# A hybrid decoder step on one core: pooling projection ahead of the last o group, narrow last pooled group, reordered ends of stages

## What is computed

```
n1 = rmsnorm(h); q,f,v,g,u = split(n1 @ w_in)            # 5 x 1024 columns
o  = rmsnorm(hgrn2(silu(q), sigmoid(f), v)) * silu(g)    # 8 heads, state 128x128 each
pm = (window_means(u) - u) @ w_pool * pool_scale         # 4 groups of 256 channels, windows 2/4/8/16
h  = h + concat(o, pm) @ w_out                           # 2048 x 2048
gu = rmsnorm(h) @ w_gate_up                              # 2048 x 11264
h  = h + (silu(gu[:5632]) * gu[5632:]) @ w_down          # 5632 x 2048
e  = rmsnorm(p @ w_ple); h = h + sigmoid(h @ w_ple_gate) * e
y  = rmsnorm(h)                                          # and the new states and pooling buffers
```

## Time and profile before

| what | value |
| --- | --- |
| three runs | 1236.65, 1238.37, 1238.66 us; median 1238.37 |
| profiled execution | 1237.61 us, span 1235.7 us |
| granted TensorE clock, mean | 0.996 of full |
| PE busy | 1198.0 us, 97% |
| DVE busy | 786.2 us, 64% |
| ACT busy | 598.5 us, 48% |
| chain that ended last, by engine | PE 89%, DVE 6%, ACT 2%, DMA 2% |
| DMA | 232.86 MB, mean 188 GB/s |

### The profile page before, as it was taken

How to read it: one execution, slowest core, us unless ns; L and a number is a source line. 1 busy time by engine, 2 the same in 40 slices (tenths; PEclk the granted TensorE clock), 3 DMA queues, 4 the chain that set the end, 5 groups by cost and what they waited for, 6 DMA issues and landing times.

```text
span 1235.7 us, 27526 instructions
## 1 busy us (share of the span) xinstructions
PE 1198.0 (97%) x10761; PEld 1039.7 (84%) x10761; DVE 786.2 (64%) x1147; ACT 598.5 (48%) x741; POOL 27.8 (2%) x41
## 2 busy tenths in 40 slices
PE   4999999999999999999999999999999999999995
PEld 2889889888888878888888888888888888888885
DVE  3657767777867866565656656565664545455686
ACT  5643453445445665555555555555443434343442
POOL 2010101100000000000000000000000000000000
PEclk9999999999999999999999999999999999999998
DMA  5664756765556567565565756566364646555551
GB/s 195 210 200 151 228 157 201 223 183 168 198 170 219 155 204 222 168 217 190 185 220 159 221 166 218 189 186 221 136 240 158 216 170 217 175 205 190 191 144 71
DMA packets 172310, 232.86 MB, mean 188 GB/s; under 512 B 10178, under 2 KB 110761, under 8 KB 171976
## 3 DMA queue, kind: packets, MB, share of 16 engines
q1 hardware_dynamic: 167728, 220.30, 55.0%
q0 software_dynamic: 3024, 10.09, 2.8%
q10 hardware_dynamic: 1504, 1.70, 0.4%
HBM read 225.08 MB, written 7.43 MB: 188 GB/s over the span
## 4 chain that ended last, share of the span: by engine, by line
PE 89%; DVE 6%; ACT 2%; DMA 2%; issue 1%; DVEq 0%; ACTq 0%; SPq 0%
PE acc L1333 28%; PE acc L1335 28%; PE acc L1337 28%; DVE lo L768 2%; PE wrk L1443 2%; DMA raw<-in_w_in_dram 1%; ACT hi L506 1%; PE wrk L1360 1%; ACT big L543 0%; DVE hid L1212 0%; DMA raw<-in_w_gate_up_dram 0%; DVE nrm L1168 0%; DVE hid L1259 0%; DMA xe<-in_x_sample_dram 0%; PE wrk L1428 0%
## 5 line engine op out<-in xcount | busy, mean ns | idle before, releaser
L1333 PE MATMUL acc<-nrm,hi 128*128 128x264 f16 x2304 | 637.3, 277 | 3.8 <-DVE tg L1174 2.3
L768 DVE SCALAR_TENSOR_TENSOR lo<-raw,hi 128x1024 f16<-128x1024 f32 x414 | 497.2, 1221 | 222.4 <-ACT hi L506 219.0
L1335 PE MATMUL acc<-nrm,hi 128*128 128x264 f16 x2304 | 637.3, 277 | 0.0
L1337 PE MATMUL acc<-nrm,lo 128*128 128x264 f16 x2304 | 637.2, 277 | 0.0
L506 ACT ACTIVATE hi<-raw 128x1024 f16<-128x1024 f32 x414 | 423.8, 1051 | 327.4 <-PE acc L1337 111.1
L1333 PEld LDWEIGHTS acc<-nrm,hi 128*128 128x128 f16 x2304 | 227.5, 99 | 38.1 <-DVE tg L1174 2.6
L1337 PEld LDWEIGHTS acc<-nrm,lo 128*128 128x128 f16 x2304 | 228.4, 99 | 32.9
L1335 PEld LDWEIGHTS acc<-nrm,hi 128*128 128x128 f16 x2304 | 228.4, 99 | 32.7
L1333 PE MATMUL acc<-big,hi 128*128 128x264 f16 x720 | 198.8, 276 | 1.5 <-DVE hid L1212 1.5
L1335 PE MATMUL acc<-big,hi 128*128 128x264 f16 x720 | 198.8, 276 | 0.0
L1337 PE MATMUL acc<-big,lo 128*128 128x264 f16 x720 | 198.8, 276 | 0.0
(11 more groups left out here) (268 smaller groups left out, 725.2 us busy)
## 6 DMA issues: line engine op xcount, KB each, us to landing
raw<-in_w_gate_up_dram SPq DMA_DIRECT2D x352, 256.0 KB, 3.9
raw<-in_w_down_dram SPq DMA_DIRECT2D x88, 512.0 KB, 4.6
raw<-in_w_in_dram SPq DMA_DIRECT2D x80, 512.0 KB, 4.5
raw<-in_w_out_dram SPq DMA_DIRECT2D x32, 512.0 KB, 4.4
raw<-in_w_ple_gate_dram SPq DMA_DIRECT2D x32, 512.0 KB, 5.0
state<-in_state_hgrn_dram POOLq DMA_DIRECT2D x8, 512.0 KB, 6.9
out_new_hgrn_sample_dram<-state POOLq DMA_DIRECT2D x8, 512.0 KB, 5.0
xe<-in_x_prompt_dram SPq DMA_DIRECT2D x2, 1024.0 KB, 7.5
```

The costliest lines, as they stand in the source:

```text
L768: stt(lo[:, st.hl_slot(j), :], raw[:, st.raw_slot(j), :], WSCALE, hi[:, st.hl_slot(j), :], ALU.mult, ALU.subtract).then_inc(lo_done, 1)
L1333: mm(out, wh, x_hi[:, kt, :], start=first, stop=False)
L1335: mm(out, wh, x_lo[:, kt, :], start=False, stop=False)
L1337: last = mm(out, wl, x_hi[:, kt, :], start=False, stop=final)
```

## The change

- The pooling projection runs after three o groups instead of four; the fourth o group follows it (`MIX_BLOCKS`, the loads, PE's streams). `POOL_AT` is block 92, it was 96.
- In the tables of the front part `OSS_AT` goes from 70 to 73, `SAMPLE_ROOT_AT` from 71 to 74, `O_MIX_AT` from (68, 70, 72, 74) to (69, 71, 73, 75), `SAMPLE_MIX_AT` from 74 to 77.
- The last pooled group is narrow with 4 blocks: each of 8 row tiles by 128 columns, each finishing one tile. DVE and ACT evict, square and sum tile by tile inside the loop.
- `square_e(i)` runs in FFN groups 1 to 16 instead of 0 to 15.
- The down pass evicts its four tiles first and converts them afterwards.
- At the end, the transposes of y go to blocks 5, 6 and 7, the last four tiles of y are transposed after the pass, the sum over the squares is made in two parts (`ya` for the first 15 tiles, `ys` for the last), the stores are cut at 768 columns instead of 960, and y_sample is stored in 32 rows of 512 columns instead of 8 of 2048.

```diff
-BUF_AT, U_LAST_AT, OSS_AT = 44, (73, 81), 70
-RMS_AT, ROOT_AT, SAMPLE_ROOT_AT = 64, 65, 71
-O_NORM_AT, O_MIX_AT, SAMPLE_MIX_AT = (66, 67, 69, 71), (68, 70, 72, 74), 74
+BUF_AT, U_LAST_AT, OSS_AT = 44, (73, 81), 73
+RMS_AT, ROOT_AT, SAMPLE_ROOT_AT = 64, 65, 74
+O_NORM_AT, O_MIX_AT, SAMPLE_MIX_AT = (66, 67, 69, 71), (69, 71, 73, 75), 77
...
-MIX_BLOCKS += [(st, 0, j) for st in S_OUT_O for j in range(4)]
+MIX_BLOCKS += [(st, 0, j) for st in S_OUT_O[:-1] for j in range(4)]
+POOL_AT = len(MIX_BLOCKS)
 MIX_BLOCKS += [(S_POOL, 0, j) for j in range(2)]
-MIX_BLOCKS += [(st, 0, j) for st in S_OUT_P for j in range(4)]
+MIX_BLOCKS += [(st, 0, j) for st in S_OUT_O[-1:] + S_OUT_P for j in range(4)]
 MIX_END = len(MIX_BLOCKS)
-POOL_AT = IN_BLOCKS + 4 * OUT_GROUPS
...
-            for i, st in enumerate(S_OUT_P):
+            for i, st in enumerate(S_OUT_P[:-1]):
                 for j in range(4):
                     load(st, 0, j, std(w_out)(i, 4 + j))
+            for j in range(4):
+                load(S_OUT_P[-1], 0, j, w_out[:, 8:16, D - COLS + j * P:D - COLS + (j + 1) * P])
...
                 if st in S_OUT_P and j == 3 and st is not S_OUT_P[-1]:
                     square_h(S_OUT_P.index(st))
+                if st is S_OUT_P[-1]:
+                    square_h(OUT_GROUPS - 1, (j,))
                 split(*MIX_BLOCKS[b + AHEAD])
...
                     out_tiles(st, S_OUT_P.index(st))
                     out_sums(S_OUT_P.index(st))
+                if st is S_OUT_P[-1]:
+                    if j == 0:
+                        dve.wait_ge(acc_free, st.tile(0, 0))
+                    out_tiles(st, OUT_GROUPS - 1, (j,))
+                    if j == 3:
+                        out_sums(OUT_GROUPS - 1, (2, 3))
                 for c in range(QUADS):
                     quad_update(c, b - QUAD_AT[c])
                 split(*MIX_BLOCKS[b + AHEAD])
+                if st is S_OUT_P[-1] and j < 2:
+                    out_sums(OUT_GROUPS - 1, (j,))
                 for c in range(QUADS):
                     quad_rest(c, b - QUAD_AT[c])
...
-            with dve.Fori(0, KT) as i:
-                group(S_FFN, i, lambda: evac_ffn(i), between=lambda n: square_e(i) if n == 2 else None)
-            with dve.Fori(KT, S_FFN.groups - 1) as i:
+            group(S_FFN, 0, lambda: evac_ffn(0))
+            with dve.Fori(1, KT + 1) as i:
+                group(S_FFN, i, lambda: evac_ffn(i), between=lambda n: square_e(i - 1) if n == 2 else None)
+            with dve.Fori(KT + 1, S_FFN.groups - 1) as i:
...
             def evac_down(i):
                 for n in range(TPG):
                     wait_tile(dve, S_DOWN, i, n)
+                    h = tile_of(h_all, i, n)
+                    stt(h, acc[:, n, 0:TOK], C_FF, h, ALU.mult, ALU.add).then_inc(acc_free, 1)
+                for n in range(TPG):
                     h, nh = tile_of(h_all, i, n), tile_of(n_hi, i, n)
-                    stt(h, acc[:, n, 0:TOK], C_FF, h, ALU.mult, ALU.add).then_inc(acc_free, 1)
                     dve.wait_ge(acc_free, S_DOWN.tile(i, n) + 1)
                     ts(nh, h, HSCALE, None, ALU.mult).then_inc(down_chain, 1)
...
             gate_tile(last_gate, 0)
             split(S_GATE, last_gate, 7)
             gained((12,))
-            y_taken(0)
-            gate_tile(last_gate, 1)
-            gained((13,))
-            for c in (1, 2):
+            for n in (1, 2):
+                gate_tile(last_gate, n)
+                gained((12 + n,))
+            for c in range(3):
                 y_taken(c)
-            gate_tile(last_gate, 2)
-            gained((14,))
-            dve.wait_ge(gate_chain, Y_LAST // P * 3)
             gate_tile(last_gate, 3, summed=False)
+            ssp = rt[:, 8:11]
+            wait_job("ya")
+            ts(ssp[:, 0:2], bank("ya")[:, 0:2], 1.0 / D, EPS, ALU.mult, ALU.add)
+            link(drain(ts(ssp[0:NSAMP, 2:3], bank("ya")[0:NSAMP, 2:3], 1.0 / D, EPS, ALU.mult, ALU.add), "ya"))
             gained((15,))
-            y_taken(3)
-            wait_job("ys_2")
-            for n in range(3):
-                m = P if n < 2 else NSAMP
-                last = drain(ts(ss[0:m, n:n + 1], bank(f"ys_{n}")[0:m, 0:1], 1.0 / D, EPS, ALU.mult, ALU.add), f"ys_{n}")
-            link(last)
+            wait_job("ys")
+            stt(ss[:, 0:2], bank("ys")[:, 0:2], 1.0 / D, ssp[:, 0:2], ALU.mult, ALU.add)
+            link(drain(stt(ss[0:NSAMP, 2:3], bank("ys")[0:NSAMP, 2:3], 1.0 / D, ssp[0:NSAMP, 2:3], ALU.mult, ALU.add), "ys"))
...
+                if i == OUT_GROUPS - 1:
+                    pe.wait_ge(pd_ready, 2)
+                    stream(S_POOL, 0, pd_hi, pd_lo,
+                           layout=lambda j, n, kk: ((n // 2 * 2 + kk) * 256 + n % 2 * P, 2 * (2 * j + n // 2) + kk))
                 stream(st, 0, m_hi, m_lo, ready=out_ready if i == 0 else None,
                        woven=lambda j: in_jobs(IN_BLOCKS + 4 * i + j))
...
-            for st in S_OUT_P:
+            for st in S_OUT_P[:-1]:
                 stream(st, 0, m_hi, m_lo, layout=lambda j, n, kk: (kk * COLS + n * P, 8 + BLOCK_KT * j + kk))
+            stream(S_OUT_P[-1], 0, m_hi, m_lo, first_row=8)
...
+            square_sums("ya", h_ssq, (KT - 1) * 3)
+            pe.wait_ge(hg_ready, KT - 1)
+            late = [job(f"yp_3_{a}") for a in range(2)]
+            for a in range(2):
+                late_y(late[a], a, range(12, 15))
+            square_sums("ys", h_sq, (KT - 1) * 3 + 2)
             pe.wait_ge(hg_ready, KT)
-            out = job("yl_0")
-            nc.tensor.transpose(out[:, 0:P], h_all[:, KT - 1, 0:P], ident[:])
-            nc.tensor.transpose(out[0:NSAMP, P:2 * P], h_all[:, KT - 1, SEQ:TOK], ident[:]).then_inc(job_done, 1)
-            nc.tensor.transpose(job("yl_1")[:, 0:P], h_all[:, KT - 1, P:SEQ], ident[:]).then_inc(job_done, 1)
+            for a in range(2):
+                late_y(late[a], a, (15,)).then_inc(job_done, 1)
+            late_y(job("yq_3"), 2, range(12, 16)).then_inc(job_done, 1)
```

More of the change, by code:

```diff
@@ L115, in tile_done @@
         if self.one_tile(i):
-            return "used", self.block(i, 2 * n + 1) + 1
+            return "used", self.block(i, (n + 1) * self.bpg // TPG - 1) + 1
         if n == TPG - 1:
@@ L124 @@
 S_OUT_O, S_OUT_P = [], []
-for _ in range(OUT_GROUPS):
+for _ in range(OUT_GROUPS - 1):
     S_OUT_O.append(Stage(S_OUT_O[-1] if S_OUT_O else S_IN, 1, 4))
 S_POOL = Stage(S_OUT_O[-1], 1, 2, closed=True)
-for _ in range(OUT_GROUPS):
-    S_OUT_P.append(Stage(S_OUT_P[-1] if S_OUT_P else S_POOL, 1, 4))
+S_OUT_O.append(Stage(S_POOL, 1, 4))
+for _n in range(OUT_GROUPS):
+    S_OUT_P.append(Stage(S_OUT_P[-1] if S_OUT_P else S_OUT_O[-1], 1, 4, narrow=_n == OUT_GROUPS - 1))
 S_PLE = Stage(S_OUT_P[-1], 1, 4, closed=True)
@@ L640, in pooled, with square_h @@
                         .then_inc(mix_hi, 1)
-            def square_h(i):
-                for n in range(TPG):
+            def square_h(i, ns=range(TPG)):
+                for n in ns:
                     act.wait_ge(acc_free, S_OUT_P[i].tile(0, n) + 1)
@@ L1061, in pooled, with out_tiles @@
                         ALU.mult, ALU.subtract).then_inc(acc_free, 1)
-            def out_tiles(st, i):
-                for n in range(TPG):
+            def out_tiles(st, i, ns=range(TPG)):
+                for n in ns:
                     wait_tile(dve, st, 0, n)
@@ L1068, in out_tiles, with out_sums @@
                     stt(h, acc[:, n, 0:TOK], C_N, h, ALU.mult, ALU.add).then_inc(acc_free, 1)
-            def out_sums(i):
-                for n in range(TPG):
+            def out_sums(i, ns=range(TPG)):
+                for n in ns:
                     dve.wait_ge(hsq_ready, i * TPG + (n + 1))
@@ L1305, in _, with stream @@
             mm = nc.tensor.matmul
[L1307 removed]
+            def stream(st, i, x_hi, x_lo, ready=None, layout=None, sigmoid_frees=False, woven=None, first_row=0):
                 for j in range(st.bpg):
@@ L1314, in stream @@
                     narrow = st.one_tile(i)
-                    for n in (j // 2,) if narrow else range(TPG):
-                        if j == 0 or st.closed or (narrow and j % 2 == 0):
+                    per = st.bpg // TPG
+                    for n in (j // per,) if narrow else range(TPG):
+                        if j == 0 or st.closed or (narrow and j % per == 0):
                             t = st.tile(i, n, j)
@@ L1331, in stream @@
                             if narrow:
-                                first, final = kk == 0 and j % 2 == 0, kk == 7 and j % 2 == 1
+                                first, final = kk == 0 and j % per == 0, kk == 7 and j % per == per - 1
                             mm(out, wh, x_hi[:, kt, :], start=first, stop=False)
@@ L1683, in _, with square_sums @@
                    woven=lambda j: y_transposes(Y_AT.index(j)) if j in Y_AT else iter(()))
-            for _ in y_transposes(3):
-                pass
-            sums = [job(f"ys_{n}") for n in range(3)]
```

(3 more changed lines are left out.)

79 lines of the change are left out of this document (39 added, 40 removed).

## The result

| | the kernel before | the change |
| --- | --- | --- |
| median beside each other | 1238.51 us | 1242.12 us (1240.44 to 1242.99) |
| ratio | | 1.0037, interval 1.0027 to 1.0047 |
| the same two kernels in a later comparison | 1237.21 us | 1243.0 us; ratio 1.0041, 1.0028 to 1.0054 |
| profiled execution, span | 1237.61, 1235.7 us | 1240.44, 1238.6 us |
| mean granted clock of it | 0.996 | 0.994 |

The medians are 3.6 us apart (0.29%); the ratio, which the comparison gives with its interval, says 0.37%, 4.6 us. Either way the change costs time, clear of the noise. The forecast was +1.05 us, no change.

A forecast was written before the change was run, and what follows sets the result against it. TensorE (PE), busy 97% of the span, bounds the kernel: time is its matmuls plus its waits. +2.0 - 1.05 + 2.9 - 0.6 - 2.0 - 0.2 = +1.05 us gave 1239.4 us on the median, range 1234.0 to 1242.2.

The forecast's parts named there:

- Head-norm jobs: Blocks 60 to 74: two waits go, 1.64 us off, but PE newly waits 3.7 us for o_sq; net +2.0 us.
- the 0.17 that the prediction adds to every other wait: Any PE wait: costs its idle time plus 0.17 us, as a row gives 0.28 us while the next starts after 0.11.
- nothing more is lost at the o pass: Start of the o pass: mixed heads ready some 0.4 us before PE comes, so no further cost counted.
- Pooling projection: Ahead of the last o group: PE's idle time falls from 2.0 to 0.95 us, a gain of 1.05 us.
- Narrow last group: Last pooled group: DVE reads the sums job 3.3 us later, 0.37 hidden; cost 2.9 us, bounds 0 and 3.3.
- the ladder: Last pooled group: add, square, two splits and sum in sequence take 3.5 us a block, where PE needs 2.70.
- Square of e: First FFN group (part 4): last weight block issued earlier without the 0.9 us square ahead; gain 0.6 us, between 0 and 0.9.
- Down pass: Down pass: evicting all four tiles first removes three 0.5 us waits, 3 x (0.5 + 0.17) = 2.0 us off.
- The end: Kernel's end: wait grows from 1.0 to 2.6 us, +1.4, then -0.8, -0.7, -0.1; together -0.2 us, bounds -1.0 and +1.0.
- rival A: Behind the new 3.7 us wait: PE's clock falls to half pace, costing 1.8 us; 1241.2 us, chance 0.2.
- D: Rival: gains from pooling order, square of e and end don't come, 1.85 us more; 1241.2 us, chance 0.07.
- slower: Whole kernel: slower by over 0.2%, above 1240.8 us, from rivals A, D and the forecast range's top; chance 0.25.

The follow-up runs named there:

- osq_early: The early square: the change with o_sq made in DVE's block 70 instead of 72, nothing else; 1242.53 us, ratio 1.0039 against the kernel before.
- both: The change with o_sq in block 70 and the last pooled group wide as before; 1237.2 us against 1237.23 for the kernel before, ratio 0.9998.
- best_oldend: The change with head-norm tables, wide last pooled group and end as before; 1233.09 against 1237.21 us, ratio 0.9964; once more 1233.77 against 1236.69, ratio 0.9970.
- fill: The change with 30 thrown-away matmuls on PE before its wait for o_sq; 1237.07 us against 1236.96 for the kernel before, ratio 1.0000.
- fill_both: As fill, plus 2 and 9 thrown-away matmuls at waits starting the embedding pass; 1237.4 us against 1237.5 for the kernel before, ratio 1.0002.
- end_only: The kernel before with only the end changed; ratio 1.0011 (1.0002 to 1.0020), +1.4 us.
- down_only: The kernel before with only the down pass changed, all four evictions first; ratio 0.9985 (0.9976 to 0.9994), -1.9 us.
- head_old: The change with the head-norm tables of the kernel before, all else as changed; 1237.83 us against 1236.96 for the kernel before, ratio 1.0004.

## Why the prediction was wrong

Point by point, each against its own step:

1. **Head-norm jobs: the stand right, the fall behind it left out.** The wait of 3.7 came as 3.5. The stretch lost 3.69 us, and without the fall 1.96 (+2.0 forecast; with the 0.17 that the prediction adds to every other wait it would have been +2.2). That nothing more is lost at the o pass held. The early square shows that this rested on the same wait: without it, 3.2 us of another appear, and in `both`, without a fall, blocks 60 to 80 together take 1.66 us more than before.
2. **Pooling projection: right.** -1.10 for -1.05, in every profile with this order.
3. **Narrow last group: right without the fall.** +2.75 for +2.9, the ladder link by link. With a fall +3.98. Here I counted the ladder link by link and never asked what PE's clock does behind the short waits that it makes.
4. **Square of e: the earlier issue came, the earlier landing didn't.** The first FFN group took 23.6 to 25.2 us over the profiles of all kernels, and two profiles of the very same kernel lie 1.4 apart (23.64 and 25.08, `best_oldend`). The chain through this group ends in the load of a weight block, and the difference is in that load. Start and length of it, in the first and the second of these profiles:

```profile
423.49 4.97 DMA raw<-in_w_gate_up_dram
423.94 6.41 DMA raw<-in_w_gate_up_dram
```

With the move, the chain comes to this load 8.44 us after DVE's last scaling of an FFN input (13 profiles, 0.01 apart; 8.90 and 9.18 in `fill` and `fill_both`), without it 9.22 (5 profiles). These 0.78 us are what part 4 counted on. But the load then takes 4.2 to 6.5 us, 5.6 in the mean, where it takes 4.6 to 5.7 without the move, 5.0 in the mean. The stretch is 24.4 us in the mean either way. So the profiles give the part nothing; timed alone it gave 1.4 (0.2 to 2.5), and from where stays open.
5. **Down pass: right, undersized.** 2.53 us for three waits, 0.84 each instead of 0.67. The 0.17 that I added to each idle time were 0.3 here.
6. **The end: right without the fall.** From block 403 to the end the profile shows -0.15 for -0.2. That is less than executions differ there without a fall (old end 49.42 to 50.10 us in 8 profiles, new end 49.27 to 49.72 in 6; the means are 0.2 apart). But the wait of 2.5 us, which the sum had at its own length (2.6), brought a fall of 1.6 us in 6 of 12 profiles that have it, and in none of 8 with the wait of 1.0.

The step that failed is thus rival A: the half pace of PE behind a new wait was left out of the sum and put at a chance of 0.2, for one wait only. Behind the wait on `o_sq` it came in 3 of 3 profiles and cost 1.73 us, 1.8 forecast. The price was right partly by luck: it took 4.0 us of low clock at 0.20 us a matmul from the earlier trace rows, where the fall has some 15 matmuls 0.22 us apart, 3.3 us, and the two slips nearly cancel. The chance was argued from the 2.3 us wait that showed no fall, and the prediction itself said that the rival decides if the wait comes near its full length. It forecast that full length in the same sum, and the wait came at 3.5 of 3.7. And the rival was tied to one wait, where four places of this kernel (the head norm, the starts of the embedding and FFN passes, the last gate group) showed a fall. (The chances don't add up either: A and D alone are 0.27, both above 1240.8, and "slower" was given 0.25.)

By the stretches the change without any fall is 1.96 - 1.10 + 2.75 - 2.65 = +0.96 us, plus what the first FFN group adds (0.73 here); with the two falls of the first profile +3.9. The medians say +3.6 and +5.8, the ratios +4.6 and +5.1. That 0.96 lies so near the forecast of 1.05 is luck as well: the same parts were forecast at +1.65, and the 0.6 that part 4 should give didn't come. The Trainium skill (TensorE: Matmul & The Clock Gate, HAM oscillation), by which each such wait pays the warm-up again, agrees with the first place; that the fall also comes behind waits of 2.3 to 3.2 us in one execution and not in the next, the runs show beyond it.

One more thing stood on a single profile: the FFN wait of 2.3 us, without a fall, that spoke against rival A. In the kernels that change nothing ahead of it or in it, it was 2.1 (`end_only`) and 2.8 us (`down_only`), and at 2.8 a fall follows it. The kernel before is the same program up to there, so it should have this fall in a part of its executions too; no profile of it shows that.

What stays open: why the fall at the embedding pass comes in some executions (5 of 7 profiles that have its waits as in the change; `osq_early` and `head_old` don't show it); why waits of the same length bring a fall in one execution and not in the next; why work in the first stand lowered the number of later falls; and why the load in the first FFN group takes 4.2 us once and 6.5 another time.

## What to carry to other kernels

Cost a new wait of PE twice: by its own length, and by the pace of PE behind it. Here the second was 1.0 to 1.7 us a time, more than most of the edits were worth. One wait of 3.5 us with its fall cost more than three of 1.1 far apart would (an estimate: 3.5 + 0.17 + 1.73 = 5.4 against 3 x 1.27 = 3.8; none of the 10 profiles with a lone wait of 1.1 us on `o_sq` has a fall behind it). A list of waits doesn't show it; the granted clock by stretch does, and the mean clock of each execution (0.997, 0.994, 0.991) sorts the executions of one program by it, if roughly. Before moving a table of dependent jobs by some blocks, follow the last of them, not the first: putting only the first back won nothing.
